# A GpSimd angle table in four tiles, with per-partition scalars in place of broadcast operands

## The reference

```
lam_bar = jnp.exp(lam * dt)                       # one complex number for each group and state
bu = jnp.einsum('bsgc,gpc->bsgp', u, b_bar)
a = jnp.broadcast_to(lam_bar, bu.shape)
_, h = lax.associative_scan(combine, (a, bu), axis=1, reverse=reverse)   # h_t = a h_(t-1) + bu_t
return jnp.einsum('bsgp,gcp->bsgc', h, c).real
y = s5_direction(forward) + s5_direction(reverse) + d * u
y = gelu(y);  y = y * sigmoid(y @ w_glu + b_glu)
```

## Time and profile before

| | us |
|---|---|
| median of 3 runs (lowest to highest) | 2341.74 (2336.95 to 2351.07) |
| the profiled execution, its own time | 2340.44 |
| its span | 2338.7 |
| TensorE busy | 2287.4 |
| VectorE busy | 1361.5 |
| ScalarE busy | 990.1 |
| GpSimd busy | 176.1 |

### The profile page before, as it was taken

One profiled execution on the slowest core, in us unless ns is written; L12 is line 12 of the kernel. 1 busy time (PEld: TensorE's weight loads), 2 busy tenths in 40 slices (PEclk: granted clock), 3 DMA queues, 4 the chain that ended last, 5 costly groups with the idle time before them and its releaser, 6 DMA issues.

```text
span 2338.7 us, 31322 instructions
## 1 busy us (share of the span) xinstructions
PE 2287.4 (98%) x12654; PEld 1929.5 (83%) x12654; DVE 1361.5 (58%) x1495; ACT 990.1 (42%) x1338; POOL 176.1 (8%) x68
## 2 busy tenths in 40 slices
PE   8999999999999999999999999999999999999999
PEld 7887667888888888888888888878888888888887
DVE  6898846564545554444466478656545555444544
ACT  6212145443443444444454366635434344443444
POOL 0797500000000000000000000000000000000000
PEclk9999999999999999999999999999999999999999
DMA  8455334455666655565543433345566665555553
GB/s 312 126 135 140 126 108 160 158 170 177 189 191 186 191 186 198 192 241 195 198 148 130 162 109 108 100 161 169 159 191 194 181 196 185 192 195 186 193 197 108
DMA packets 153187, 400.13 MB, mean 171 GB/s; under 512 B 15232, under 2 KB 30848, under 8 KB 133008
## 3 DMA queue, kind: packets, MB, share of 16 engines
q1 hardware_dynamic: 141072, 391.98, 51.3%
q10 hardware_dynamic: 12032, 6.98, 1.3%
HBM read 396.80 MB, written 2.13 MB: 171 GB/s over the span
## 4 chain that ended last, share of the span: by engine, by line
PE 87%; DVE 8%; ACT 3%; issue 1%; ACTq 1%; DMA 1%; DVEq 0%
PE ps L706 20%; PE ps L707 10%; PE ps L746 10%; PE ps L747 10%; PE ps L748 10%; PE ps L595 5%; PE ps L611 2%; PE ps L918 2%; PE ps L920 2%; PE ps L919 2%; DVE w_low L2105 2%; PE ps L603 2%; PE ps L604 1%; PE ps L605 1%; DVE region L1918 1%
## 5 line engine op out<-in xcount | busy, mean ns | idle before, releaser
L2105 DVE TENSOR_TENSOR w_low<-raw_weights,w_high 128x1024 fp32r<-128x1024 f32 (+1 forms) x628 | 738.6, 1218 | 776.2 <-ACT w_high L1384 776.1
L1384 ACT ACTIVATE w_high<-raw_weights 128x1024 fp32r<-128x1024 f32 (+1 forms) x628 | 628.5, 1049 | 818.5 <-PE ps L748 402.2
L706 PE MATMUL ps<-x_split,w_high 128*128 128x512 f32 x2048 | 718.3, 395 | 6.3 <-DVE w_low L2105 2.7
L707 PE MATMUL ps<-x_split,w_low 128*128 128x256 f32 x2048 | 573.1, 280 | 0.0
L706 PEld LDWEIGHTS ps<-x_split,w_high 128*128 128x128 f32 x2048 | 386.0, 188 | 95.9 <-issue 6.4
L746 PE MATMUL ps<-w_high,x_split 128*128 128x512 f32 x1024 | 398.6, 389 | 3.1 <-DVE w_low L2105 3.1
L748 PE MATMUL ps<-w_high,x_split 128*128 128x512 f32 x1024 | 398.4, 389 | 0.0
L747 PE MATMUL ps<-w_low,x_split 128*128 128x512 f32 x1024 | 398.4, 389 | 0.0
L707 PEld LDWEIGHTS ps<-x_split,w_low 128*128 128x128 f32 x2048 | 388.2, 190 | 0.0
L746 PEld LDWEIGHTS ps<-w_high,x_split 128*128 128x128 f32 x1024 | 192.3, 188 | 44.0 <-DVE w_low L2105 4.0
L748 PEld LDWEIGHTS ps<-w_high,x_split 128*128 128x128 f32 x1024 | 192.3, 188 | 40.0
(11 more groups left out here) (276 smaller groups left out, 2258.7 us busy)
## 6 DMA issues: line engine op xcount, KB each, us to landing
raw_weights<-in_w_ff SPq DMA_DIRECT2D x128, 1024.0 KB, 5.2
raw_weights<-in_w_up SPq DMA_DIRECT2D x64, 1024.0 KB, 5.3
raw_weights<-in_w_down SPq DMA_DIRECT2D x64, 1024.0 KB, 4.8
raw_weights<-in_w_in SPq DMA_DIRECT2D x62, 1024.0 KB, 5.4
raw_weights<-in_w_out SPq DMA_DIRECT2D x32, 1024.0 KB, 4.9
raw_weights<-in_w_mem_kv SPq DMA_DIRECT2D x8, 1024.0 KB, 13.6
region<-t_table ACTq DMA_DIRECT2D x1, 3072.0 KB, 17.0
raw_weights<-in_w_in SPq DMA_DIRECT2D x4, 768.0 KB, 4.6
```

The costliest lines, as they stand in the source:

```text
L706: nc.tensor.matmul(o, wh[:, q, w], xs[:, kt], start=(kt == 0), stop=False, skip_group_check=True)
L707: last = nc.tensor.matmul(o[:, 0:S], wl[:, q, w], xh[:, kt], start=False, stop=(kt == KT - 1), skip_group_check=True)
L1384: nc.scalar.activation(split_slot(wh_t, k)[:, r], ring_slot(n)[:, r], ACT.Copy).then_inc(rounded, 1)
L2105: V.tensor_tensor(split_slot(wl_t, k)[:, r], ring_slot(n)[:, r], split_slot(wh_t, k)[:, r].bitcast(f32), ALU.subtract).then_inc(split_read ...
```

## The change

Each of GpSimd's steps is done for one tile of 128 x 256 at a time, in a loop over the four tiles of a chunk. The three products of the time steps with a column, which had both operands broadcast in a tensor_tensor, become tensor_scalar with the column as the scalar of each partition. Adding `MAGIC`, which shared an instruction with the subtraction, now shares one with the first product; the subtraction stands alone. The values computed are the same. `turns` of a chunk is named four times, and the last naming counts.

```diff
-            time = iota.unsqueeze(1).to_broadcast([P, 4, S])
             for i in range(CHUNKS):
-                col = lambda k: ssm[k][:, 4 * i:4 * i + 4].unsqueeze(2).to_broadcast([P, 4, S])
                 if i:
                     pool.wait_ge(act_done, at("turned_in", i - 1))
-                m.did(nc.gpsimd.tensor_tensor(tmpb, time, col(8), ALU.mult))
-                m.own()
-                m.did(nc.gpsimd.tensor_scalar(tmpb, tmpb, MAGIC, MAGIC, ALU.add, ALU.subtract))
-                m.did(nc.gpsimd.tensor_tensor(turns, time, col(10), ALU.mult))
-                m.own()
-                m.did(nc.gpsimd.tensor_tensor(turns, turns, tmpb, ALU.subtract))
-                m.own()
-                m.did(nc.gpsimd.tensor_tensor(tmpb, time, col(11), ALU.mult))
-                m.own()
-                m.did(nc.gpsimd.tensor_tensor(turns, turns, tmpb, ALU.add))
-                m.own()
-                m.did(nc.gpsimd.tensor_scalar(turns, turns, 0.5, -0.5, ALU.min, ALU.max), "turns", i)
+                for q in range(4):
+                    turn, tmp = turns[:, q], tmpb[:, q]
+                    col = lambda k: ssm[k][:, 4 * i + q:4 * i + q + 1]
+                    m.did(nc.gpsimd.tensor_scalar(tmp, iota, col(8), MAGIC, ALU.mult, ALU.add))
+                    m.did(nc.gpsimd.tensor_scalar(turn, iota, col(10), None, ALU.mult))
+                    m.own()
+                    m.did(nc.gpsimd.tensor_scalar(tmp, tmp, MAGIC, None, ALU.subtract))
+                    m.own()
+                    m.did(nc.gpsimd.tensor_tensor(turn, turn, tmp, ALU.subtract))
+                    m.own()
+                    m.did(nc.gpsimd.tensor_scalar(tmp, iota, col(11), None, ALU.mult))
+                    m.own()
+                    m.did(nc.gpsimd.tensor_tensor(turn, turn, tmp, ALU.add))
+                    m.own()
+                    m.did(nc.gpsimd.tensor_scalar(turn, turn, 0.5, -0.5, ALU.min, ALU.max), "turns", i)
```

## The result

The changed kernel takes 2407.97 us (median of 4 runs, 2396.64 to 2411.10) against 2340.46 us of the kernel before (also 4 runs): 1.0268 times as long, 95% interval 1.0244 to 1.0293. The profiled execution has a span of 2408.1 us, 69.4 more than before. When the same kernel was measured again later beside the kernel before on one chip, it took 2399.07 us against 2344.82, 1.0246 times (1.0217 to 1.0275). So the change costs some 2.5 to 2.7%, near 60 us.

The account below looks back on a forecast made before the run. PE holds the end, with POOL's table a chain with 17.2 us of slack; POOL's cycle of 20.4 + 9 + 2.1 = 31.5 us makes PE 47 us late, so 2340.4 + 47 = 2388 us, range 2341 to 2431.

Parts of the forecast that it names:

- forecast path: From POOL's last table, 9.2 us on ACT and DVE to PE's L855, due at 276.2; PE 47 us late.
- (a): On POOL, two tensor_tensor per tile stay, at 0.72 us each on 256 elements.
- (b): On POOL, the clamp of each tile stays, at 0.40 us on 256 elements.
- (c): On POOL, multiply by a column and add MAGIC in one tensor_scalar: 1.04 us a tile, bounds 0.40 and 1.04.
- (d): On POOL, three one-operation tensor_scalar per tile (multiply, subtract, multiply): 0.61 us each, bounds 0.40 and 1.04.
- Rival 1: One-input work on POOL is cheap, running at the clamp's rate: PE 7 to 30 us late; chance 0.25.
- (e): POOL and DVE taking turns gets dearer with small instructions: 9 us a chunk, ends 5.4 and 10.9.
- The sum: First table 67.33 to 93.7, seven cycles of 31.5 to 314.2, plus 9.2 gives 323.4: PE 47 us late.
- the bias loads: ACT's 16.7 us of issuing behind the fourth table end near 208 us, before the fifth (220): covered.
- the slack of 17.2 us: Between POOL's last table and PE's deadline at L855, 17.2 us were said to hide a slower POOL.
- Rival 2: Not slower: POOL 15.4 us a chunk, turns still 5.4, cycle 22.9, result 2339 to 2345; chance 0.12.
- Rival 3: Small POOL instructions cost more than their elements: 25.6 us a chunk, cycle 36.7, PE 89 us late; chance 0.17.

Follow-up runs that it names:

- experiment 4: Changed kernel with only the three products tile by tile, the rest 1024 wide, and all scalar forms as multiply-add: 2341.69 us, 0.9987 times the kernel before.
- 5, one clamp more: Kernel before with one more clamp of `turns` in each chunk: 2344.70 us, 1.0003 times the kernel before.
- 7, four more: Kernel before with four more clamps of `turns` in each chunk: 2381.89 us, 1.0156 times the kernel before.
- 1, old forms by tile: Kernel before with its old instruction forms cut into tiles of 128 x 256, 28 instructions a chunk: 2387.39 us, 1.0194 times the kernel before.
- experiment 2: Changed kernel with its three one-operation tensor_scalar written as multiply and add: 2362.64 us, 1.0099 times the kernel before.
- 3, products by tile: Changed kernel with only the three products tile by tile; subtraction, two tensor_tensor and clamp 1024 wide: 2361.27 us, 1.0082 times the kernel before.
- experiment 6: Kernel before with two more clamps of `turns` in each chunk: 2357.13 us, 1.0055 times the kernel before.
- experiment 8: Changed kernel without DVE's four products that turn the scanned states back: 2371.97 us, 1.014 times the kernel before.
- experiment 9: Kernel before with two more clamps a chunk, and ACT writing decay 3 before issuing the bias loads: 2354.44 us, 1.0042 times the kernel before.
- experiment 11: Changed kernel unedited, measured again beside the kernel before on one chip: 2399.07 us, 1.0246 times the kernel before.
- 10: Changed kernel with ACT writing decay 3 before issuing the bias loads: 2398.60 us, 1.0232 times the kernel before.
- 12: Changed kernel with decay 3 ahead of the bias loads, repeated beside the unedited changed kernel: 2402.69 us, 1.0255 times the kernel before.

## Why the prediction was right

It said 2388 us, 2341 to 2431, and slower with a chance of 0.67. The chain of steps held; sizes were off, and two of the errors cancelled in part.

*The bound and the path.* The claim was that PE holds the end, has 1.7 us to give, and that POOL's table is a second chain with a slack. Experiments 4, 5 and 7 show all three: less POOL work gives nothing, a little more can't be told in the time, more than that is paid. The forecast path (last table, 9.2 us on ACT and DVE, PE's L855 at 276.2) can be checked in every profile:

| kernel | last table out | + 9.2 - 276.2 | L855 late by | time over before |
|---|---|---|---|---|
| changed | 321.1 | 54.1 | 54.8 | 67.5 |
| 1, old forms by tile | 309.0 | 42.0 | 42.6 | 44.3 |
| 2, multiply-add by tile | 282.7 | 15.7 | 16.7 | 19.6 |
| 3, products by tile | 281.2 | 14.2 | 14.8 | 18.2 |
| 5, one clamp more | 254.7 | none | 2.3 | 1.9 |
| 6, two more | 270.8 | 3.8 | 11.8 | 14.4 |
| 7, four more | 297.8 | 30.8 | 31.4 | 39.1 |
| 8, no turning back | 294.4 | 27.4 | 28.0 | 29.2 |
| 9, as 6, decay first | 274.4 | 7.4 | 8.9 | 8.3 |

Where the sum gives 14 us or more it holds to 1 us. Where it gives less (5, 6, 9), PE was late before it came to the last table. In 2, 3, 7 and 8 PE also met an earlier place, the one behind the bias loads, and waited 9.9, 8.5, 10.7 and 14.7 us for DVE there; by the sum it would have been about as late at the last table without it.

*(a), (b)*: 0.72 and 0.40 us, measured 0.722 and 0.399. *(c)*: taken at 1.04, measured 0.475, near the lower bound. *(d)*: taken at 0.61, measured 0.92, 0.85 and 0.93, towards the upper one. The two errors have opposite signs, and that is luck: a tile takes 5.42 us against 5.11. By the prediction's own sum, (c) right alone would have given some 30 us late and (d) right alone some 75 (estimates from these rows). This was the weakest step. "Half of L1897's arithmetic" assumed that two operations cost twice one, and experiments 2 and 3 show the reverse: multiply-add is the cheap pair and one operation the dear case. Rival 1 (one-input work at the clamp's rate) is true of the pair and false of the single form. The rule of the Trainium skill ("GPSIMD Engine Reference", "Engine selection") that was quoted with it, one-input work at roughly line-rate, fares the same: the pair measured 0.83 ns an element, the single form 2.50.

*(e)*: taken at 9 us a chunk, measured 8.5, with experiment 8 showing the partner; the upper end, 10.9, was not reached. The cycle was 32.3, forecast 31.5. The first table took 27.7 us (67.1 to 94.8), forecast 26.4.

*The sum*: seven cycles of 32.3 in place of 31.5 (5.8 us) and a first table 1.3 longer, begun 0.2 earlier, give the 54.1 in place of 47; L855 comes 0.7 later still, and another 2 come from PE's lower clock at the end. That makes 57. The mis-sized term is (d) net of (c), some 10 us over eight tables; (e), half a microsecond a cycle too large, took some 3.5 back. The rest of the first comparison, up to 67.5, lies behind 344 us, where the same kernel was some 14 us shorter in experiment 11; in that comparison it is 54.3 over the kernel before. The forecast had that stretch unchanged, so this part of the miss is in none of its terms.

*A step that was wrong, and cost nothing here*: the bias loads were called covered, since they end near 208 us and the fifth table comes at 220. The comparison was with the wrong successor. Directly behind the loads on ACT stands decay 3, and DVE wanted it from 203 us in the changed kernel: its scan waited 7.93 us and PE's L842 5.55. Here that delay lies on the way to a later, larger one (experiments 10 to 12); in experiment 6 it is what is paid, and the slack of 17.2 us is too large there. The slack at the seventh table is also smaller than at the last: in experiment 9 the seventh is out at 247.5, and L842, which waits for `yev` behind its scan, starts at 266.99, 19.5 us later; before, 226.9 + 19.5 left 13.4 us up to 259.79.

*Rival 2* fell, since neither the forms nor the turns came near the 24.7 us a cycle from which it decides. (By the description given with it, 22.99 plus a seventh of 17.2 - 2.5, that limit is 25.1; with 32.3 measured it changes nothing.) *Rival 3* fell too: the fixed part is 0.19 to 0.21 us, near the 0.18 taken, and the form with a pointer operand takes 0.07 more (0.475 against 0.407 in experiment 2).

## What to carry to other kernels

Before splitting an instruction of a helper engine, multiply the fixed part and the gap by the new number of instructions, and ask whose turn it must wait for. Small instructions can meet more of the other engine's: here the turns taken rose from 5.4 to 8.5 us a chunk, and even where the work itself shrank (experiment 4) they ate the saving. An engine that looks half idle on the page can stand a few microseconds a cycle from the critical path; its slack is read at every place where its product is wanted, not at the last one alone, and what stands directly behind a late instruction on each queue has to be looked up. A form's price has to come from a row of that form, since more operations in one instruction may cost less.

## What was not expected of the hardware

On GpSimd, tensor_scalar with multiply and add takes 0.475 us on 128 x 256 with a pointer for the first scalar, 0.407 with two constants, and 1.047 on 128 x 1024: 0.83 ns an element, as fast as the clamp (0.84). With one operation, multiply or subtract, it takes 0.85 to 0.93 us and, on 1024, 2.775: 2.50 ns an element. Add and subtract in one instruction cost 3.34 ns an element (1.068 and 3.631 us). Why a single operation is three times as dear as this pair no run here shows.
